# 64 bytes in front of the activations' operands: every tile behind them starts at a multiple of 128 bytes

## The reference

```python
def first_block(x, ...):
    h = rms_norm(x, norm_mix[l]);  u = h @ w_in[l]                     # 1024 -> 2560
    hl = rg_lru(causal_depthwise_conv(lru_x), ...)                     # gated recurrence over time
    y_lru = gelu(lru_g) * hl
    y_att = stick_breaking_attention(q, k, v)                          # 8 heads of 64
    x = x + concat(rms_norm(y_lru), rms_norm(y_att)) @ w_out[l]
    gu = rms_norm(x, norm_ffn[l]) @ w_ffn_in[l]                        # 1024 -> 2 x 2816
    x = x + (silu(gu[:, :2816]) * gu[:, 2816:]) @ w_ffn_out[l]         # 2816 -> 1024
    return rms_norm(x, norm_final)

def second_block(x, ...):
    proj = rms_norm(x) @ w_in                                          # three conv inputs, q, k, v, f, gates
    y_conv = (cb * causal_dwconv(cc * cin)) @ w_out_conv
    y_attn = forgetting_attention(q, k, v, log_sigmoid(f + b)) @ w_out_attn
    x = x + (g_conv * y_conv + g_attn * y_attn) @ w_o
    up = causal_dwconv(rms_norm(x) @ w_up);  a, b = split(up)          # 1024 -> 2 x 2816
    x = x + (silu(a) * b) @ w_down
    return rms_norm(x)
```

## Time and profile before

| | us |
|---|---|
| median of 3 runs | 1256.82 (1256.21 to 1257.33) |
| the profiled execution | 1255.6 |
| its span, first to last instruction | 1253.8 |
| PE busy | 1228.0 (98%) |
| PEld busy | 1078.1 (86%) |
| DVE busy | 991.8 (79%) |
| ACT busy | 670.4 (53%) |
| POOL busy | 186.0 (15%) |
| TensorE clock granted, mean | 0.998 |

### The profile page before, as it was taken

One profiled execution on the slowest core, in us unless ns is written; L12 is line 12 of the kernel. 1 busy time (PEld: TensorE's weight loads), 2 busy tenths in 40 slices (PEclk: granted clock), 3 DMA queues, 4 the chain that ended last, 5 costly groups with the idle time before them and its releaser, 6 DMA issues.

```text
span 1253.8 us, 19172 instructions
## 1 busy us (share of the span) xinstructions
PE 1228.0 (98%) x7804; PEld 1078.1 (86%) x7804; DVE 991.8 (79%) x1196; ACT 670.4 (53%) x837; POOL 186.0 (15%) x168
## 2 busy tenths in 40 slices
PE   6999999999999999999999999999999999999997
PEld 5778677889999999997899999657888999988886
DVE  6888764888788778887989967566678899989886
ACT  5463674374545445567545535363444666656555
POOL 5003001002222101110122113000000222202020
PEclk9999999999999999999999999999999999999999
DMA  5423201249999779664599857301324799968765
GB/s 172 143 68 98 70 1 34 84 123 194 177 208 184 142 204 248 141 123 118 111 210 197 190 101 206 113 1 34 117 86 151 125 213 194 183 157 173 207 116 137
DMA packets 144458, 174.14 MB, mean 139 GB/s; under 512 B 5370, under 2 KB 118250, under 8 KB 144242
## 3 DMA queue, kind: packets, MB, share of 16 engines
q0 software_dynamic: 58288, 71.33, 35.7%
q1 hardware_dynamic: 86066, 101.58, 24.3%
q10 hardware_dynamic: 16, 0.00, 0.0%
HBM read 170.78 MB, written 2.11 MB: 138 GB/s over the span
## 4 chain that ended last, share of the span: by engine, by line
PE 92%; DVE 4%; ACT 2%; issue 1%; DMA 0%; SPq 0%; ACTq 0%; DVEq 0%
PE psum L2516 12%; PE psum L2522 12%; PE psum L2519 12%; PE psum L2785 11%; PE psum L2783 11%; PE psum L2784 11%; PE psum L2857 3%; PE psum L2859 3%; PE psum L2858 3%; PE psum L3065 2%; PE psum L3066 2%; PE psum L3067 2%; PE psum L2974 1%; PE psum L2660 1%; PE psum L2645 1%; PE psum L2672 1%
## 5 line engine op out<-in xcount | busy, mean ns | idle before, releaser
L990 ACT ACTIVATE w_hi<-raw 128x1024 fp32r<-128x1024 f32 (+2 forms) x121 | 156.2, 1294 | 210.5 <-PE psum L2522 145.6
L1544 DVE TENSOR_TENSOR w_lo<-raw,w_hi 128x1024 fp32r<-128x1024 f32 (+2 forms) x121 | 184.4, 1526 | 57.2 <-ACT w_hi L990 57.2
L2516 PE MATMUL psum<-act_hi,w_hi 128*128 128x512 f32 x520 | 207.7, 399 | 4.3 <-DVE act_lo L1551 1.5
L2522 PE MATMUL psum<-act_hi,w_lo 128*128 128x512 f32 x520 | 204.7, 394 | 0.1
L2519 PE MATMUL psum<-act_lo,w_hi 128*128 128x512 f32 x520 | 203.6, 391 | 0.0
L2785 PE MATMUL psum<-s_hi,w_lo 128*128 128x256 f32 x704 | 194.9, 277 | 0.0
L2783 PE MATMUL psum<-s_hi,w_hi 128*128 128x256 f32 x704 | 194.8, 277 | 0.0
L2784 PE MATMUL psum<-s_lo,w_hi 128*128 128x256 f32 x704 | 194.8, 277 | 0.0
L2785 PE MATMUL psum<-act_hi,w_lo 128*128 128x256 f32 x528 | 146.2, 277 | 0.0
L2783 PE MATMUL psum<-act_hi,w_hi 128*128 128x256 f32 x528 | 146.1, 277 | 0.0
L2784 PE MATMUL psum<-act_lo,w_hi 128*128 128x256 f32 x528 | 146.1, 277 | 0.0
(11 more groups left out here) (411 smaller groups left out, 2672.6 us busy)
## 6 DMA issues: line engine op xcount, KB each, us to landing
raw<-in_w_in SPq DMA_DIRECT2D x15, 1024.0 KB, 5.4
xz<-in_w_ffn_in POOLq DMA_DIRECT2D x24, 512.0 KB, 6.6
raw<-in_w_ffn_in SPq DMA_DIRECT2D x22, 512.0 KB, 5.5
xz<-in_w_up POOLq DMA_DIRECT2D x21, 512.0 KB, 6.1
raw<-in_w_up SPq DMA_DIRECT2D x18, 512.0 KB, 5.2
raw<-in_w_in SPq DMA_DIRECT2D x16, 512.0 KB, 5.0
v<-in_w_in POOLq DMA_DIRECT2D x15, 512.0 KB, 6.2
x_buf<-in_w_ffn_out POOLq DMA_DIRECT2D x6, 1024.0 KB, 9.8
```

Of the source, the lines that this page charges most:

```text
L990: A(w_at(w_hi, s, h, n - h), home(s, n)[:, h:n], ACT.Copy).then_inc(w_hi_ready, 1)
L1544: V.tensor_tensor(w_at(w_lo, s, h, n - h), home(s, n)[:, h:n], w_at(w_hi, s, h, n - h).bitcast(F32), ALU.subtract).then_inc(w_lo_ready, 1)
L2516: ins = mm(dst, stationary[0], moving[0], start=first, stop=False)
L2522: return mm(dst, stationary[1], moving[0], start=False, stop=last)
```

## The change

One tile of 16 float32 columns, 64 bytes per partition, is allocated between gain_both and the point where `act_base` is read. Nothing reads or writes it. act_hi, act_lo and all tiles that are allocated behind them or placed from `act_base` start 64 bytes later; what lies in front stays where it is. The instructions, their order, their shapes and their waits are the same.

```diff
@@ -404,6 +404,7 @@
         f_bias = sb("f_bias", [HEADS, 1])
         eps = sb("eps", [P, 2])
         gain_both = sb("gain_both", [P, DC])
+        sb("act_pad", [P, 16])
         act_scope = ExitStack()
         act_base = nc.sbuf_base
         act_hi = sb("act_hi", [P, DC, TOKENS], F32R, act_scope)
```

## The result

The changed kernel takes 1283.28 us (median of 4 runs, 1281.8 to 1285.35) against 1256.78 us for the kernel before beside it (1256.21 to 1257.33): a ratio of 1.0212, 95% interval 1.0194 to 1.023, so 26.5 us slower. The forecast was 1253.9 us with a range of 1247 to 1269; the sign was wrong, and the time lies outside the range.

A forecast was written before the change was run, and what follows sets the result against it. The prediction took TensorE's chain of matmuls, one behind the other, as the bound. From the median of 1256.8 us it took 2.9 for the 654 w-moving matmuls and 0 for all else: 1253.9 us, range 1247 to 1269.

The forecast's parts named there:

- the two paces: fp32r matmul steps at either width come at two paces some 4.5 ns apart: 228.8 and 233.4, 113.5 and 117.8.
- the slow w-moving stages: Lines 3065 to 3067 and V slabs, weights moving: about 233 ns a step, blamed on the stationary operand lying 64 off.
- The term of -2.9 us: 654 matmuls with weights moving each get 4.5 ns back once their stationary operand is at a multiple of 128.
- zero for the 6468 w-stationary matmuls: Products with stationary weights, 1848 of 512 columns and 4620 of 256: moving operand's new offset taken to change nothing.
- a bound of 29 us on either side: For the 6468 products with stationary weights: one pace up or down, +-4.5 ns each, +-29 us.
- The suffix sum: soft moving, neg stationary, both 64 off: ten steps in 1.50 us, 2 ns a step over the fast pace.
- Rival 1: All matmul steps: offset does nothing, paces depend on how a stream starts; 1256.8 us, or 1253; chance 0.28.
- Rival 2: Products with stationary weights: equal positions cost 2 ns a step, 12.9 us lost, 1268 us; chance 0.15, plus 0.08 towards 1286.
- deciding point of 0.8 ns a step: Price per w-stationary product at which Rival 2 decides: 6468 x 0.8 = 5 us, more than the 2.9 won.
- Rival 2's far end of 1286: A moving operand at a multiple of 128 itself costs 4.5 ns on 6468 products, 29 us; chance 0.08.
- Rival 3: Moving operand's offset costs as well, so w-stationary products get faster: up to 29 + 2.9 us, 1225; chance 0.12.
- The stretch at 619 to 714 us: Some 806 steps of 256 columns at the slow pace, 3.6 us; taken as unchanged.

The follow-up runs named there:

- e1: Kernel before with 64 unused bytes in front of xT, so weights and act both move and keep their distance: 1260.54 us, ratio 1.0027.
- e3: Kernel before with 128 unused bytes in front of act_hi, instead of the change's 64: 1275.55 us, ratio 1.0143.
- e6: Kernel before with 192 unused bytes in front of act_hi, so act and weights lie at equal places modulo 256: 1275.47 us, ratio 1.0134.
- e4: Kernel before with 32 unused bytes in front of act_hi: 1289.0 us, ratio 1.0253.
- e10: Kernel before with wider w_hi and w_lo, and the 55 full weight slabs for 512-column products written 64 bytes later: 1266.22 us, ratio 1.0063.
- e11: Kernel before with w_lo alone beginning 192 bytes later, all else in place modulo 256: 1267.31 us, ratio 1.0078.
- e12: Kernel before with wider w_hi and w_lo, and only the 25 slabs in which weights move written 64 bytes later: 1254.67 us, ratio 0.9988.
- e7: Kernel before with 256 unused bytes in front of act_hi, instead of the change's 64: 1256.56 us, ratio 0.9989.

## Why the prediction was wrong

**Right: what to read.** The path is one fp32r matmul behind the other, the step is what changes, and ScalarE's splits (1057 and 1055 ns) and the plain float32 products (618 ns) feel nothing of the offset. All of this held, and no transfer is seen to hold TensorE up. So did the two paces, and that a stream can fall into the slow one and stay there.

**Wrong: the cause of the slow w-moving stages.** The prediction took the offset of the stationary operand by itself as what the earlier trace rows pay for. e1 moves that offset to a multiple of 128 and the step stays at 233.3; e3 leaves it off the multiple and the step falls to 229.4. The cause is the distance, -64 modulo 256. The prediction had the distance in hand ("in rows 5 and 6 it is the other way round") and read from it only which of the two operands is off a multiple, not how far and to which side one lies from the other. The term of -2.9 us came out as -1.0: from -64 to 128 is 233.3 to 232.4, not to 228.9.

**Wrong, and the step that decided: zero for the 6468 w-stationary matmuls.** The prediction had no full stage at the new distance and took 0. Measured, the term is 24.3 + 0.7 + 5.9, together 30.9 us, a mean of 4.8 ns for each of the 6468: they left d = +64, which had the fast steps, for 128, which has slower ones at both widths. The prediction kept a bound of 29 us on either side, but 0.08 of chance for its upper end and a range that ended at 1269.

**The suffix sum could not decide it.** It was the one row at d = 128 (soft is at 192 and neg_tri at 64 modulo 256), and it showed 2 ns a step over the fast pace. Those ten steps are one head of eight. First and last start of the same ten steps of another head in the kernel before, and of the head of the earlier trace rows in e6, where the suffix sum has d = +64:

```profile
144.75 0.46 PE L2672 MATMUL psum<-soft_hi,neg_ones 128*128 128x384 f32 x2
146.29 0.27 PE L2672 MATMUL psum<-soft_lo,neg_tri 128*128 128x256 f32 x1
150.69 0.45 PE L2673 MATMUL psum<-soft_hi,neg_ones 128*128 128x384 f32 x2
152.20 0.28 PE L2673 MATMUL psum<-soft_lo,neg_tri 128*128 128x256 f32 x1
```

That is 1.54 and 1.51 us. Over the first seven heads (the eighth has a gap inside) the ten steps take 1.50 to 1.54 us at d = 128 (before), 1.50 to 1.53 at +64 (e6) and 1.50 to 1.54 at -64 (after). So this stage, of changing widths, does not show the distance at all, and that its 2 ns point the way the change went is luck.

**The rivals.** Rival 1 is wrong: the offset does something, 2.1% here. The rule of the Trainium skill beside it (SBUF — State Buffer, Specifications (TRN2)), 16-byte cachelines with a cost for crossing into a new one, would leave every run here alike, since all paddings are multiples of 16 bytes. e3, e4 and e6 differ by up to 13.5 us from each other, so for fp32r operands the runs decide otherwise; for ScalarE's splits, which have not changed, they agree. Rival 2 was right in sign and in looking at where one stream lies relative to the other; it passed its deciding point of 0.8 ns a step. Its price was too low, 2 ns against 4.8 (6.4 at 256 columns, 3.2 at 512), and came from the suffix sum, which shows no price. Equal positions are not the bad case as such: with d = +96 e4 is the slowest layout, and d = 0 and d = 128, both equal modulo 128, differ by 5 ns at 512 columns (227.4 and 232.4). Rival 2's far end of 1286 was near the number, but by a reason that e1 refutes (a moving operand at a multiple is not itself slow). Rival 3 is wrong in sign, though right that 228.8 is no floor: d = 0 gives 227.4.

**The stretch at 619 to 714 us,** taken as unchanged, lost about 1 ns a step (342 to 339 in the window); it was spared because it had been in the slow pace already. Had it been fast, the change would have cost some 816 x 4.5 ns = 3.7 us more.

**What it should have been.** With d of each pair written out modulo 256 there were two kinds of full stage in the profile of before: +64 (fast, or slow for a stretch) and -64 (slow). All 6468 w-stationary matmuls stood at the only distance at which a full stage was fast, and the change takes every one of them away from it, to a distance that no full stage had. That gives no time, but a sign to weigh: no row showed a faster step than theirs, and a slower one stood in the earlier trace rows. The bound of 29 us to the slow side deserved more than the 0.23 of chance that rival 2 had in all.

**Still open:** why these distances and not others give the short steps; what chooses between the two paces that several distances have; whether the 256-column stages of e3 were slow by their distance or by that choice; why e10 gets the slow one; and what sets the step where the high and low parts lie at different places, as in e11.

## What to carry to other kernels

Read the step between matmul starts for each pair of operands and write beside it the start of the moving minus the start of the stationary operand, modulo 256 bytes and with its sign; padding in front of a group of tiles changes that number for every pair across the padding, and "aligned" is not what fp32r matmuls want. When only a short stage already has the new arrangement, read every repetition of it before it is used for or against the change; where they differ by more than the effect, it says nothing, and the whole bound stays open. Time such a change stage by stage by the steps, because a stretch that falls into another pace at a gap moves the total by more than the change is worth.

## What the runs showed of the hardware

- A 256-column fp32r matmul at full granted clock starts 113.3 to 120.0 ns after the one before, a 512-column one 227.3 to 234.3, depending on where its two operands lie relative to each other, and at several distances on which of two paces the stretch is in. From the best to the worst layout of the same program the time goes from 1254.7 (e12) to 1289.0 us (e4).
- The pattern has a period of 256 bytes: 128 more changes it (e3, 1275.55 us), 256 more does not (e7, 1256.56 us). At 512 columns it knows the sign: +64 is 229.1 to 229.4 in the mean and -64 is 233.3 ns. At 256 columns +64 and -64 have the same two paces, 113 and 117.8.
- One layout can hold two paces. In e1 the step went from 113 to 118 ns at a gap of 0.49 us at 1021.7 us and stayed there for the rest of the stage, and in e12 the same at one of 0.37 us at 696.5 us. A gap alone does not do it: at gaps of 0.44 us (657.4 us) and 0.38 us (1002.3 us) in e1 the step stayed at 113.3. The kernel before entered its slow stretch at 618.3 us at once, without a gap.
- Plain float32 matmuls (618 ns) and ScalarE's split (1055 to 1057 ns) showed nothing of it in their durations. Nor did the fp32r suffix sum, of changing widths, in its steps (1.50 to 1.54 us for ten at d = 128, +64 and -64).
